# Sample attention laid out token-major on column strips, and deviations by Ln and Exp, in a hybrid encoder layer

## The chip, the cores and the metric

The kernel runs on one core of a Trainium2 chip. The metric is the device time of one launch in microseconds (us), the median of several runs. TensorE does the matrix products, VectorE, ScalarE and GpSimd the elementwise work, SyncE issues most of the transfers.

## What is computed

One layer of a hybrid encoder for 512 prompt tokens and 32 sample tokens, which share the weights. The parts that the change touches are these:

```
mod = silu(c) @ w_ada + b_ada          # c: 2 rows (prompt, sample); w_ada 1024 x 6144
a   = rmsnorm(h)*(1+sc1) + sh1 ;  a @ w_in -> retention q,k,v,gate and stick-breaking q,k,v
# stick-breaking attention, 4 heads of 128, sample: 32 queries on 1024 cached + 32 own keys
z = q.k / sqrt(128);  keep = log_sigmoid(-z), 0 where masked
A = exp(log_sigmoid(z) + sum of keep over the later keys);  out = A @ v
ret = groupnorm(retention out) * g * silu(gate)
h = h + gt1 * (concat(ret, out) @ w_out);   b = rmsnorm(h)*(1+sc2) + sh2;   then PEER(b)
```

PEER is a feed-forward part with 16384 experts and takes most of the time; the change doesn't touch it.

## The kernel before

Every engine has its own program, and semaphores order them. All activations lie feature-major (128 features on the partitions, 544 tokens along the row). A product in full precision is either fp32, which the trace shows as two instructions for each matmul, or, for the three big projections (`gemms[0]`, w_in; `gemms[1]`, w_out; `gemms[2]`, the query weights), three fp32r products of a high and a low part of weights (`whi`, `wlo`) and activations (`XH`, `XL`). GpSimd casts the high part of a weight chunk, VectorE subtracts to get the low part (`lo`). `gemm_start` works chunk 0 and 1 row block by row block, as the blocks of `XH`, `XL` become ready.

**Start.** w_ada comes in 12 groups of 512 columns. Groups 0, 2, 3 and 4 are multiplied on TensorE (`ada`, L599): 8 fp32 matmuls, whose stationary side is `siluT`, 128 rows by 2 columns, all accumulated on partitions 0 and 1. ScalarE copies the two rows (`ada_row`), and four products with `sel4` (`ada_turn`) turn them onto the partitions. Groups 1 and 5 to 11 are summed on VectorE, 16 instructions each (`ada_chunk`), and a product with ones adds the partitions (`ada_columns`). The first `gemm_start` needs the shifts and scales of groups 0 to 3, the reciprocal deviation `rs`, and the first chunk of w_in, whose load waits in the queue of SyncE for the place of group 1 (`wraw` slot 0). `ada(3)`, group 4, stands on TensorE ahead of `gemm_start`.

**Stick-breaking attention.** Prompt and sample share the engines. For a prompt head, `sb_z` makes scores, `softplus` (ScalarE: Abs, Exp, Ln) and `masked` (VectorE) make log keeps, `sb_sums` adds the suffix sums by products with a triangular matrix and with minus ones, `least` masks the diagonal, `weights` takes exponentials, `sb_out` multiplies with the values, `result` evicts. There is one tile of weights, `aw`, so `weights(h)` waits for `sb_out(h-1)`. The sample's scores lie key-major: `sample_z` makes 32 products of 32 columns, in pieces between the heads; `sample_own` the own keys. Its softplus is done once, on ScalarE ahead of `weights(3)`; then VectorE sums blocks (`rsum`), TensorE does 24 products for the suffix sums (L878 to L882), ScalarE the exponentials, and 36 products with 128 stationary columns and 32 moving ones give the output (L890). Only behind these comes `gemm_start(gemms[1])`.

**Deviations.** The group norm of retention and both RMS norms take Sqrt on ScalarE and `reciprocal` on VectorE (L1678 once for each head, L1602, L1768). The tables of ScalarE are changed from Sqrt to Ln and Exp ahead of the heads.

Of the kernel before, what the change touches and what calls it, by code (L numbers as in the profile page):

```python
# [22 lines left out]
P = 128  # L23
# [95 lines left out]
def build(nc, x_prompt, x_sample, c_prompt, c_sample, state_ret, cache_sb_k, cache_sb_v, w_ada, b_ada, norm1_g, w_in,  # L119
# [21 lines left out]
    siluT = at("siluT", o + 896, [KD, 2])  # L141
# [30 lines left out]
    sel4 = at("sel4", RT + 29184 + 640, [2])  # L172
    rows = at("rows", RT + 20480, [P])
# [6 lines left out]
    aw = at("aw", A0 + 20480, [1, 1280])  # L180
# [138 lines left out]
    s_w = [sem("s_w0"), sem("s_w1")]  # L319
    s_rowsT_ps, s_rowsT = sem("s_rowsT_ps"), sem("s_rowsT")  # L320
# [17 lines left out]
    for name, groups, reads in (("in", 7, 1), ("out", 2, 3), ("qry", 4, 1)):  # L338
# [56 lines left out]
    def _(sp):  # L395
# [22 lines left out]
        ada_load(1, 0)  # L418

        def adaw_load(g):  # L420

            if not isinstance(g, int) or g > 4:

                sp.wait_ge(*((s_ada_mm, 4) if isinstance(g, int) and g == 5 else (s_adas, 16 * (g - 4))))
            sp.dma_start(adaw[:], w_view(w_ada, g)).then_inc(s_adaw, 16)

        def gemm_loads(st, w, first_waits):

            for slot in range(2):
                sp.wait_ge(*first_waits[slot])  # L430
                sp.dma_start(wraw[:, slot], w_view(w, slot)).then_inc(s_w[slot], 16)
# [137 lines left out]
    def _(pe):  # L569
# [24 lines left out]
        def ada(n, par, w):  # L594

            if n >= 2:
                pe.wait_ge(s_adar, n - 1)
            for k in range(KD):
                last = mm(PS[0:2, 4 + par, :], siluT[:, k, :], w[:, k, :], start=(k == 0), stop=(k == KD - 1))  # L599
            last.then_inc(s_ada_mm, 1)  # L600

        def ada_turn(n, par, bank, col):

            pe.wait_ge(s_adar, n + 1)
            for x in range(4):
                last = mm(PS[:, bank, bass.ds(col + 2 * x, 2)], adar[0:2, par, x * P:(x + 1) * P], sel4[0:2, :],
                          start=True, stop=True)
# [81 lines left out]
        def gemm(st):  # L689

            def group(g, slot, first=0):
                for cc in range(first, 4):
# [4 lines left out]
                    if st is gemms[0] and cc == 1:  # L697
                        ada_columns(g + 1, slot, 7, 8 * g)
# [45 lines left out]
        ada_columns(8, 1, 7, 56)  # L744
# [69 lines left out]
        pe.wait_ge(s_gsd, NH)  # L814
# [4 lines left out]
        def sb_z(h):  # L819
            if h >= 2:  # L820
                pe.wait_ge(s_bev, h - 1)
            for kb in range(QB):
# [16 lines left out]
        def sb_out(h):  # L839
            pe.wait_ge(s_ba, 7 * (h + 1))  # L840
            for kb in range(QB):
                last = mm(zb(h, 0, kb * P, TP), svt[:, kb, h * P:(h + 1) * P],
                          aw[:, 0, pcol(kb):pcol(kb) + TP - P * kb], start=(kb == 0), stop=(kb == QB - 1))
            last.then_inc(s_bo, 1)

        def sample_z(b0):
            for b in (b0, b0 + 1):
                for h in range(NH):
                    mm(PS[:, 6 + b // 4, (b % 4) * P + h * TS:(b % 4) * P + (h + 1) * TS], kT[:, h, b * P:(b + 1) * P],
                       projT[:, SQ + h, TP:T], start=(b % 4 == 0 and h == 0), stop=(b % 4 == 3 and h == NH - 1),  # L850
                       skip_group_check=True)

        def sample_own():
            for h in range(NH):
                last = mm(PS[0:TS, 2, 256 + h * TS:256 + (h + 1) * TS], projT[:, SK + h, TP:T], projT[:, SQ + h, TP:T],
                          start=False, stop=(h == NH - 1), skip_group_check=True)
            last.then_inc(s_cz, 1)
            pe.sem_inc(gemms[1].mm, CREDIT)
# [3 lines left out]
        sample_z(0)  # L862
        sample_z(2)
        sb_sums(0)
        for h in range(NH):
            if h < 2:
                sample_z(4 + 2 * h)
            sb_out(h)
            if h < NH - 2:
                sb_z(h + 2)  # L870
            if h == NH - 2:
                sample_own()
            if h < NH - 1:
                sb_sums(h + 1)
        pe.wait_ge(s_clk, 1)
        for b in range(NPB):
            out = PS[:, 6 + b // 4, (b % 4) * P:(b % 4 + 1) * P]
            mm(out, ntri, lks[:, b, :], start=False, stop=False, skip_group_check=True)  # L878
            if b < NPB - 1:
                mm(out, negones[:], rsum[:, b, :], start=False, stop=False, skip_group_check=True)  # L880
            mm(out, negones[:], lks[:, NPB, :], start=False, stop=True, skip_group_check=True)
        mm(PS[0:TS, 2, 256:256 + P], ntri[:, 0:TS], lks[:, NPB, :], start=False, stop=True,  # L882
           skip_group_check=True).then_inc(s_cc, 1)
        pe.wait_ge(s_ca, 2)
        pe.wait_ge(s_vc, 16)
        for h in range(NH):
            hs = slice(h * P, (h + 1) * P)
            for b in range(NPB + 1):
                lhs = vraw[:, b, hs] if b < NPB else svt[:, 4, hs]
                last = mm(PS[:, 4, h * TS:(h + 1) * TS], lhs, aws[:, b, h * TS:(h + 1) * TS], start=(b == 0),  # L890
                          stop=(b == NPB))
        last.then_inc(s_co, 1)
# [178 lines left out]
    def _(act):  # L1071
# [9 lines left out]
        def squares(st, ready, b, rows=0):  # L1081
# [10 lines left out]
            act.wait_ge(st.ss, 1)  # L1092
            act_(halves(rs[:]), pair(b), ACT.Sqrt, bias=epsc[:, 0:1], scale=1.0 / D).then_inc(st.sd, 1)

        def ada_row(n, par):
# [4 lines left out]
            act_(adar[0:2, par, :], PS[0:2, 4 + par, :], ACT.Copy).then_inc(s_adar, 1)  # L1100
# [50 lines left out]
        act_(siluT[:].rearrange("p k g -> p g k"), rowsT[:, 0:16].rearrange("p (g k) -> p g k", g=2),  # L1151
# [4 lines left out]
        ada_row(2, 0)  # L1156
        for k in range(KD):
            act.wait_ge(norms[0].scaled, 2 * k + 2)
            act_(XH[:, k, :], scr1[:, k, :], ACT.Copy).then_inc(norms[0].hi, 1)
        ada_row(3, 1)  # L1160
# [28 lines left out]
        for h in range(NH):  # L1189
            act.wait_ge(s_gcen, h + 1)  # L1190
            act_(sqb[:, h, :], projT[:, h, :], ACT.Square).then_inc(s_gsq, 1)
        for h in range(NH):
            act.wait_ge(s_gv, h + 1)
            act_(halves(rsb[:, h, :]), pair(2 * h), ACT.Sqrt, bias=epsc[:, 0:1]).then_inc(s_gsd, 1)


        nc.scalar.preload_act_table_set("natural_log_exp_and_others")

        def softplus(h):
# [3 lines left out]
            if h >= 2:  # L1203
                act.wait_ge(s_bo, h - 1)
# [859 lines left out]
```

## Time and profile before

| | |
|---|---|
| median of 3 runs | 1860.61 us (1857.23 to 1862.22) |
| profiled execution | 1858.28 us, span 1856.5 us |
| instructions | 30125 |
| PE, PEld, DVE, ACT, POOL busy | 1771.3, 1697.8, 1426.0, 835.3, 564.4 us |

The span lacks 1.8 us of the execution's time, which lie around it. Times in rows are us from the start of the span. PE is TensorE's matmul side, PEld its weight loads, DVE VectorE, ACT ScalarE, POOL GpSimd, SPq the queue of SyncE.

### The profile page before, as it was taken

The numbers are of one execution on the slowest core, as the hardware profiler recorded it, in microseconds if no ns is written. First come the engines' busy times: TensorE is split into PE (matmuls) and PEld (weight loads), VectorE is DVE, ScalarE is ACT, GpSimd is POOL, SyncE is SP. The second block draws the span as 40 slices with busy tenths as digits, with TensorE's granted clock in tenths as the row PEclk, the third lists the DMA queues.
The fourth block names the chain that finished last, engine by engine and source line by source line (L and its number), as shares of the span: only waits on it lengthen the run. The fifth ranks groups of instructions, "written<-read, shape, count | busy, mean of one in ns | idle before, by whom it ended". The sixth has DMA issues, their size and how long they took to land.

```text
span 1856.5 us, 30125 instructions
## 1 busy us (share of the span) xinstructions
PE 1771.3 (95%) x11794; PEld 1697.8 (91%) x11794; DVE 1426.0 (77%) x2656; ACT 835.3 (45%) x1144; POOL 564.4 (30%) x442
## 2 busy tenths in 40 slices
PE   6999999797999999999999989998999999999998
PEld 2899986697999999999999989998899999999997
DVE  6667755435358998879878898686388988889997
ACT  2112135312125555554545545454465555555555
POOL 0111100011111524333543345434334434434320
PEclk9999999798999999999999999999999999999999
DMA  8545331032116979999999989999789999999983
GB/s 307 208 167 178 109 130 57 9 124 73 46 46 207 344 250 319 316 312 306 344 337 326 332 286 353 360 370 355 282 295 381 386 402 384 392 389 384 394 337 115
DMA packets 189217, 497.20 MB, mean 268 GB/s; under 512 B 13436, under 2 KB 76504, under 8 KB 180760
## 3 DMA queue, kind: packets, MB, share of 16 engines
q1 hardware_dynamic: 133704, 293.72, 44.4%
q0 software_dynamic: 55376, 201.61, 29.3%
q8 instruction: 91, 1.49, 0.3%
q14 instruction: 46, 0.38, 0.1%
HBM read 443.90 MB, written 51.12 MB: 267 GB/s over the span
## 4 chain that ended last, share of the span: by engine, by line
PE 82%; DVE 8%; DMA 6%; ACT 3%; issue 1%; POOL 0%; SPq 0%; DVEq 0%; ACTq 0%
PE PS L1019 24%; PE PS L574 13%; PE PS L576 12%; PE PS L575 12%; PE PS L636 5%; PE PS L970 4%; PE PS L944 3%; DMA vrw<-in_peer_v_dram 2%; DVE gat L1824 2%; DMA uraw<-in_peer_u_dram 2%; DMA gat<-in_peer_u_dram,idx 1%; PE PS L599 1%; PE PS L615 1%; PE PS L890 1%; PE PS L645 1%
## 5 line engine op out<-in xcount | busy, mean ns | idle before, releaser
L1464 POOL DMA_INDIRECT gat<-in_peer_v_dram,idx x192 | 255.1, 1329 | 368.0 <-DVE acc L1845 335.5
L1464 POOL DMA_INDIRECT gat<-in_peer_u_dram,idx x192 | 246.3, 1283 | 387.0 <-DVE a L1824 312.5
L574 PE MATMUL PS<-XH,uth 128*128 128x352 f32 x1024 | 341.6, 334 | 0.0
L1019 PE MATMUL PS<-wh,vh 128*128 128x352 f32 x1024 | 333.8, 326 | 7.6 <-DVE wl L1965 3.2
L1019 PE MATMUL PS<-wl,vh 128*128 128x352 f32 x1024 | 331.2, 323 | 0.0
L575 PE MATMUL PS<-XL,uth 128*128 128x352 f32 x1024 | 330.3, 323 | 0.0
L576 PE MATMUL PS<-XH,utl 128*128 128x352 f32 x1024 | 330.0, 322 | 0.0
L1019 PE MATMUL PS<-wh,vl 128*128 128x352 f32 x1024 | 329.6, 322 | 0.0
L1845 DVE SCALAR_TENSOR_TENSOR acc<-gat,a,acc 128x1024 f32<-128x1024 f32 x184 | 233.8, 1280 | 31.6 <-PE PS L576 27.3
L1824 DVE CUSTOM_DVE_ANT_0 gat<-gat,x 128x1024 f32<-128x1024 f32 x192 | 231.9, 1219 | 25.1 <-DMA gat<-in_peer_u_dram,idx 25.0
L574 PE MATMUL PS<-XH,whi 128*128 128x272 f32 x784 | 229.7, 293 | 10.3 <-DVE XL L1773 7.9
L576 PE MATMUL PS<-XH,wlo 128*128 128x272 f32 x784 | 228.7, 292 | 0.0
L575 PE MATMUL PS<-XL,whi 128*128 128x272 f32 x784 | 227.0, 290 | 0.0
L1329 ACT ACTIVATE vh<-vrw 128x1024 fp32r<-128x1024 f32 x128 | 135.9, 1061 | 201.0 <-PE PS L1019 182.6
L1289 ACT ACTIVATE utl<-PS 128x1024 fp32r<-128x1024 f32 x128 | 131.4, 1026 | 170.7 <-PE PS L944 170.7
L1019 PEld LDWEIGHTS PS<-wh,vh 128*128 128x128 f32 x1024 | 192.6, 188 | 11.5 <-DVE vl L1963 8.2
L1963 DVE TENSOR_TENSOR vl<-vrw,vh 128x1024 fp32r<-128x1024 f32 x128 | 156.6, 1224 | 60.0 <-ACT vh L1329 59.6
L575 PEld LDWEIGHTS PS<-XL,uth 128*128 128x128 f32 x1024 | 193.7, 189 | 5.5
L1435 POOL CAST whi<-wraw 128x1024 fp32r<-128x1024 f32 x49 | 56.0, 1145 | 469.0 <-PE PS L576 309.3
L574 PEld LDWEIGHTS PS<-XH,uth 128*128 128x128 f32 x1024 | 193.4, 189 | 5.5
L576 PEld LDWEIGHTS PS<-XH,utl 128*128 128x128 f32 x1024 | 193.2, 189 | 0.0
L1019 PEld LDWEIGHTS PS<-wl,vh 128*128 128x128 f32 x1024 | 192.7, 188 | 0.0
(294 smaller groups left out, 3182.7 us busy)
## 6 DMA issues: line engine op xcount, KB each, us to landing
uraw<-in_peer_u_dram SPq DMA_DIRECT2D x128, 512.0 KB, 5.8
vrw<-in_peer_v_dram SPq DMA_DIRECT2D x64, 1024.0 KB, 7.4
acts_dram<-gel SPq DMA_DIRECT2D x128, 176.0 KB, 6.5
gates_dram<-gst SPq DMA_DIRECT2D x22, 1024.0 KB, 10.4
al<-acts_dram SPq DMA_DIRECT2D x32, 704.0 KB, 10.4
G<-gates_dram SPq DMA_DIRECT2D x32, 704.0 KB, 9.4
adaw<-in_w_ada_dram SPq DMA_DIRECT2D x9, 2048.0 KB, 7.9
wraw<-in_w_in_dram SPq DMA_DIRECT2D x7, 2048.0 KB, 7.9
```

The source lines that it names most:

```text
L574: mm(out, ah, bh, start=start, stop=False)
L575: mm(out, ah, bl, start=False, stop=False)
L576: return mm(out, al, bh, start=False, stop=stop)
L636: last = mm(PS[:, k // 4, (k % 4) * P:(k % 4 + 1) * P], uraw[:, m % 2, k * P:(k + 1) * P], ident, start=(k % 4 == 0), stop=(k % 4 == 3), i ...
L970: last = mm(PS[:, 4 + gi % 2, x * P:(x + 1) * P], ohA[:, gi % 2, x, :], ohB[:, gi % 2, x, :], start=True, stop=True)
L1019: last = mm(PS[:, k, 0:TD], v_, w_[:, j % 2, :], start=(j == 0 and n == 0), stop=(j == NU - 1 and n == 2))
L1289: act_(utl[:, m % 2], PS[:, 0:2, :].rearrange("p b (k i) -> p (b k) i", i=P), ACT.Copy).then_inc(s_utl, 1)
L1329: act_(vh[:, j % 2], vrw[:, j // 2 % 2, j % 2, :], ACT.Copy).then_inc(s_vh, 1)
L1464: nc.gpsimd.indirect_dma_start(out=gat[:, n % NGAT, :], out_offset=None, in_=table, in_offset=bass.IndirectOffsetOnAxis(ap=idx[:, k:k + 1] ...
L1824: nc.vector.tensor_tensor_reduce(gat[:, n % NGAT, :], gat[:, n % NGAT, :], x[:], 1.0, 0.0, ALU.mult, ALU.add, a[:, k:k + 1]).then_inc(s_do ...
L1845: stt(a, row, w, old, ALU.mult, ALU.add).then_inc(s_dot, 1)
L1963: tt(vl[j % 2][:], vrw[:, j // 2 % 2, j % 2, :], f(vh[:, j % 2]), ALU.subtract).then_inc(s_vl, 1)
```

## The change

- Modulation on strips: `siluT` is 32 columns wide (30 of them zero), matmul k goes to partitions 32(k mod 4) on, and `sel4` adds the four strips when it turns. Groups 0 to 4 are all done on TensorE; group 2 has a place of its own (`adax`), loaded at the start; the 16 VectorE instructions of group 1 and its `ada_columns` are gone. Group 4's product moves behind `gemm_start`. The first w_in group is loaded in halves, ahead of it only group 3 waits in the queue. The low parts of the first two weight chunks are made before the shifts are ready.
- Sample attention: token-major, head h on partitions 32h on. The cached scores are 8 fp32 products of 512 columns, 4 heads on 4 strips. The suffix sums are one VectorE scan of 1056 columns, from the last key to the first. The weights are turned by 9 transposes; the output is 36 products on strips (32 stationary columns, 128 moving) and one transpose. All is placed between prompt heads 1 and 3.
- `aw` is two tiles; the copy `XH[0:4]` moves from ScalarE to GpSimd, ahead of the casts of w_out.
- The deviations of the group norm and of the second RMS norm become Ln and an Exp with scale -0.5; their reciprocals are gone. The first RMS norm keeps its own.

```diff
@@ start, SyncE @@
+        sp.dma_start(adax[:], w_view(w_ada, 2)).then_inc(s_adax, 16)
...
-        sp.wait_ge(s_xT, 5)
-        adaw_load(2)
         sp.wait_ge(s_ada_mm, 1)
         ada_load(3, 1)
-        sp.wait_ge(s_ada_mm, 2)
-        adaw_load(4)
-        gemm_loads(gemms[0], w_in, ((s_adas, 16), (s_ada_mm, 3)))
+        gemm_loads(gemms[0], w_in, ((s_ada_mm, 2), (s_ada_mm, 4)))
@@ start, TensorE @@
-                last = mm(PS[0:2, 4 + par, :], siluT[:, k, :], w[:, k, :], start=(k == 0), stop=(k == KD - 1))
+                q = k % 4 * 32
+                last = mm(PS[q:q + 32, 4 + par, :], siluT[:, k, :], w[:, k, :], start=(k < 4), stop=(k >= 4))
...
+        pe.wait_ge(s_w[0], 16)
+        ada(1, 1, wraw[:, 0])
+        ada_turn(0, 0, 6, 0)
         sum_once(norms[0], 1, 0)
-        pe.wait_ge(s_adaw, 16)
-        ada(1, 1, adaw)
-        ada_turn(0, 0, 6, 0)
+        pe.wait_ge(s_adax, 16)
+        ada(2, 0, adax)
+        ada_turn(1, 1, 6, 8)
         pe.wait_ge(s_w[1], 32)
-        ada(2, 0, wraw[:, 1])
-        ada_turn(1, 1, 6, 16)
-        ada_columns(1, 0, 6, 8)
-        ada_turn(2, 0, 6, 24)
-        pe.wait_ge(s_adaw, 32)
-        ada(3, 1, adaw)
+        ada(3, 1, wraw[:, 1])
+        ada_turn(2, 0, 6, 16)
+        ada_turn(3, 1, 6, 24)
         pe.wait_ge(norms[0].sd, 1)
         gemm_start(gemms[0], chunk_by_chunk(norms[0].lo, 0, lambda k: k + 1))
-        ada_turn(3, 1, 7, 0)
+        pe.wait_ge(s_adaw, 16)
+        ada(4, 0, adaw)
+        ada_turn(4, 0, 7, 0)
         gemm(gemms[0])
@@ heads, TensorE @@
-        pe.wait_ge(s_gsd, NH)
...
+        def sample_z():
+            pe.wait_ge(s_gln, NH)
...
+            for b in (1, 0):
+                if b == 0:
+                    pe.wait_ge(s_cte, 1)
+                for h in range(NH):
+                    last = mm(PS[h * TS:(h + 1) * TS, 6 + b, :], projT[:, SQ + h, TP:T],
+                              kT[:, h, b * 512:(b + 1) * 512], start=True, stop=True)
...
+                    last = mm(PS[h * TS:(h + 1) * TS, 7, 0:P], aws[:, b, h * TS:(h + 1) * TS],
+                              vraw[:, b, hs] if b < NPB else svt[:, 4, hs], start=(b == 0), stop=(b == NPB),
...
         sb_z(0)
         sb_z(1)
-        sample_z(0)
-        sample_z(2)
+        sample_z()
         sb_sums(0)
-        for h in range(NH):
...
-        pe.wait_ge(s_clk, 1)
...
+        sb_sums(1)
+        sb_out(0)
+        sb_out(1)
+        sample_turn()
+        sb_z(2)
+        sample_turn_own()
+        sb_z(3)
+        sample_out()
+        sb_sums(2)
+        pe.sem_inc(gemms[1].mm, CREDIT)
+        pe.wait_ge(s_cte, 4)
+        nc.tensor.transpose(PS[:, 6, 0:P], outs[:], ident).then_inc(s_ct, 1)
+        sb_sums(3)
+        sb_out(2)
+        sb_out(3)
@@ heads, ScalarE @@
         softplus(0)
         softplus(1)
+        softplus_sample()
         weights(0)
+        act.wait_ge(s_gln, NH)
+        act_(rsb[:], rsb[:], ACT.Exp, scale=-0.5).then_inc(s_gsd, 1)
+        weights(1)
         result(0)
+        act.wait_ge(s_cmin, 1)
+        act_(sws[:], sws[:], ACT.Exp).then_inc(s_ca, 1)
+        result(1)
+        softplus(2)
+        softplus(3)
+        weights(2)
...
@@ heads, VectorE @@
         masked(0)
+        dve.wait_ge(s_cz, 1)
+        nc.vector.tensor_copy(ownz[:], PS[:, 6, 0:TS]).then_inc(s_cte, 1)
         masked(1)
         least(0)
+        link(stt(sp8, z8, 0.0, sp8, ALU.max, ALU.add),
...
+        link(nc.vector.tensor_tensor_scan(sws[:, ::-1], ones[:, 0:1].to_broadcast([P, NS_K]), sps[:, ::-1], 0.0,
+                                          ALU.mult, ALU.add))
+        least(1)
...
+        scaled(0)
         scaled(1)
+        nc.vector.tensor_copy(aws[:, 0:NPB, :], PS[:, 6:8, :].rearrange("p b (c x) -> p (b c) x", x=P)).then_inc(s_cte, 1)
+        scaled(2)
+        nc.vector.tensor_copy(aws[0:TS, NPB, :], PS[0:TS, 6, 0:P]).then_inc(s_cte, 1)
+        scaled(3)
         masked(2)
+        dve.wait_ge(s_co, 1)
+        nc.vector.tensor_copy(outs[:], PS[:, 7, 0:P]).then_inc(s_cte, 1)
         masked(3)
         for c in range(2):
             lo(gemms[1], c, 0, c)
+        least(2)
+        least(3)
@@ second norm, ScalarE and VectorE @@
+            if st is norms[1]:
+                link(act_(halves(rs[:]), pair(b), ACT.Ln, bias=epsc[:, 0:1], scale=1.0 / D))
+                act_(rs[:], rs[:], ACT.Exp, scale=-0.5).then_inc(st.sd, 1)
+                return
...
-        link(nc.vector.reciprocal(rs[:], rs[:]))
```

## Rows read from the trace of the kernel before

**Rows 1.** The page: busy us of each engine over the span.
```profile
PE 1771.3 (95%) x11794; PEld 1697.8 (91%) x11794; DVE 1426.0 (77%) x2656; ACT 835.3 (45%) x1144; POOL 564.4 (30%) x442
```

**Rows 2.** Windows: length, busy us by engine, granted clock, DMA share, GB/s.
```profile
0.00:58.30 58.30, 43.67 (x149) 17.23 (x149) 39.40 (x59) 12.36 (x19) 4.23 (x7) 0.94 0.90 325
...
437.60:443.00 5.40, 5.38 (x24) 5.40 (x25) 5.40 (x13) 2.82 (x7) 0.00 (x0) 0.50 0.01 3
```

**Rows 3.** Chain of waits, the start: start us, us, what.
```profile
19.95 9.34 DMA adaw<-in_w_ada_dram
...
48.89 9.52 PE PS L599 x16
...
70.68 0.98 PE PS L606 x8
```

**Rows 4.** Timeline, the start: start us, us, engine, instructions.
```profile
20.85 7.03 PE L599 MATMUL PS<-wraw,siluT 128*2 128x512 f32 x16 [0.93 <-DVE hT L1583]
...
28.51 9.36 DVE L1505 SCALAR_TENSOR_TENSOR adas<-wraw,siluT,adas 128x512 f32<-128x512 f32 x14
...
41.36 5.17 DVE L1604 TENSOR_TENSOR scr<-hT,rs 128x544 f32<-128x544 f32 x8
...
50.41 1.06 POOL L1435 CAST whi<-wraw 128x1024 fp32r<-128x1024 f32 x1 [49.95 <-DMA wraw<-in_w_in_dram]
...
58.34 0.39 PE L574 MATMUL PS<-XH,whi 128*128 128x272 f32 x1
```

**Rows 5.** Transfers: of 20 to 25 us; of the tile adaw.
```profile
20.00:25.00 5.00, 4.15 (x10) 0.85 (x11) 3.49 (x6) 4.10 (x8) 0.00 (x0) 1.00 1.05 387
...
DMA to landing us min/median/max: 7.9/8.2/9.3
```

**Rows 6.** Chain of waits, the heads.
```profile
287.78 2.54 ACT rsb L1194 x4
...
292.82 1.44 ACT lk L1207 x4
...
296.88 1.70 DVE lk L1692 x4
299.55 1.91 PE PS L831 x4
...
317.22 1.71 PE PS L849 x16
318.93 2.25 PE PS L842 x8
321.85 2.42 PE PS L823 x8
...
355.30 13.33 PE PS L890 x72
```

**Rows 7.** Timeline, sample attention.
```profile
312.72 0.71 PE L831 MATMUL PS<-lk,cst 128*128 128x128 f32 x3
...
332.36 0.44 PE L855 MATMUL PS<-projT 128*32 128x32 f32 x8
...
343.11 1.22 DVE L1724 SCALAR_TENSOR_TENSOR lks<-PS,lks 128x1024 f32<-128x1024 f32 x1 [4.92 <-ACT lks L1240]
...
344.71 3.81 PE L842 MATMUL PS<-aw,svt 128*128 128x512 f32 x8 [7.39 <-ACT aw L1222]
...
368.45 0.57 PE L574 MATMUL PS<-XH,whi 128*128 128x272 f32 x1
```

**Rows 8.** Timeline, the second norm.
```profile
430.50 3.55 DVE L1768 RECIPROCAL rs<-rs 128x544 f32<-128x544 f32 x1 [0.57 <-ACT rs L1093]
...
437.62 0.57 PE L574 MATMUL PS<-XH,whi 128*128 128x272 f32 x1 [7.91 <-DVE XL L1773]
```

**Rows 9.** Groups by line: count, busy us, mean ns of one.
```profile
L599 PE MATMUL PS<-wraw,siluT 128*2 128x512 f32 x32 | 14.1, 592 | 0.9 <-DVE hT L1583 0.9
...
L878 PE MATMUL PS<-lks,cst 128*128 128x128 f32 x16 | 3.1, 275 | 0.0
```

More of the change, by code:

```diff
@@ L882, in _ @@
[L882 to L891, printed above, removed]
@@ L1156, in _ @@
         ada_row(2, 0)
+        ada_row(3, 1)
         for k in range(KD):
@@ L1233, in softplus_sample @@
+            act_(sps[:, PAST:NS_K], ownz[:], ACT.Abs).then_inc(s_ach, 1)
             chain[0] += 2
             act.wait_ge(s_ach, chain[0])
-            act_(lks[:, 0:NPB, :], lks[:, 0:NPB, :], ACT.Exp, scale=-1.0).then_inc(s_ach, 1)
-            act_(lks[0:TS, NPB, :], lks[0:TS, NPB, :], ACT.Exp, scale=-1.0).then_inc(s_ach, 1)
-            chain[0] += 2
-            act.wait_ge(s_ach, chain[0])
-            act_(lks[:, 0:NPB, :], lks[:, 0:NPB, :], ACT.Ln, bias=1.0).then_inc(s_cln, 1)
-            act_(lks[0:TS, NPB, :], lks[0:TS, NPB, :], ACT.Ln, bias=1.0).then_inc(s_cln, 1)
+            link(act_(sps[:], sps[:], ACT.Exp, scale=-1.0))
@@ L1242, in _ @@
+            act_(sps[:], sps[:], ACT.Ln, bias=1.0).then_inc(s_cln, 1)
         softplus(0)
         softplus(1)
+        softplus_sample()
         weights(0)
+        act.wait_ge(s_gln, NH)
+        act_(rsb[:], rsb[:], ACT.Exp, scale=-0.5).then_inc(s_gsd, 1)
+        weights(1)
         result(0)
-        for h in range(1, NH):
-            if h < NH - 1:
-                softplus(h + 1)
-            else:
-                softplus_sample()
-            weights(h)
-            result(h)
-            if h == 2:
-                act.wait_ge(s_gy, 4)
-                act.wait_ge(s_out, 96)
-                act_(XH[:, 0:4, :], projT[:, 0:4, :], ACT.Copy).then_inc(s_ghi, 1)
@@ L1425, in group @@
                     out = whi[:, cc % 2]
-                    if cc == 0:
+                    halved = st is gemms[0] and isinstance(g, int) and g == 0
+                    if halved and cc == 0:
+                        pool.wait_ge(s_x, 48)
+                    elif cc == (2 if halved else 0):
                         pool.wait_ge(s_w[slot], 16 * (st.before[slot] + 1) + 16 * i)
@@ L1596, in _ @@
         dve.wait_ge(s_silu, 1)
-        dve.wait_ge(s_w[0], 16)
-        for k in range(KD):
-            ada_chunk(0, 0, k, wraw[:, 0])
         dve.wait_ge(norms[0].sd, 1)
@@ L1606, in _ @@
         chain[0] += 1
+        for c in range(2):
+            lo(gemms[0], c, 0, c)
         dve.wait_ge(s_adat, 4)
@@ L1619, in _ @@
                    ALU.add).then_inc(norms[0].scaled, 1)
-            if k == 1:
-                for c in range(2):
-                    lo(gemms[0], c, 0, c)
-            if k >= 2:
-                norm1_lo(k - 2)
-        norm1_lo(KD - 2)
+            if k >= 1:
+                norm1_lo(k - 1)
         norm1_lo(KD - 1)
@@ L1708, in _ @@
+        z9 = ownz[:]
+        nc.vector.memset(aws[:, NPB, :], 0.0).then_inc(s_dch, 1)
+        chain[0] += 1
+        for h in range(NH):
+            q = slice(h * TS, (h + 1) * TS)
+            stt(ownm[q, 0, :], ntri[q, q], -1.0, ident[q, q], ALU.mult, ALU.subtract).then_inc(s_dch, 1)
+            chain[0] += 1
+        dve.wait_ge(s_dch, chain[0])
+        ts(ownm[:, 1, :], ownm[:, 0, :], -NEG, NEG, ALU.mult, ALU.add).then_inc(s_zero, 1)
         masked(0)
+        dve.wait_ge(s_cz, 1)
+        nc.vector.tensor_copy(ownz[:], PS[:, 6, 0:TS]).then_inc(s_cte, 1)
```

202 lines of the change are left out of this document (105 added, 97 removed).

## The prediction

> **What bounds the kernel now.** I read the page first: PE is busy for 1771.3 of 1856.5 us [rows 1]. So time is won only where PE waits, runs at the lower clock, or does work that is taken away. The windows then show where that is, among the stages that the diff touches. Until 58.3 us PE is busy for 43.7 us, the clock is 0.94 and the transfers take 0.90 of the time; from 437.6 to 443 us the granted clock is 0.50, the lower of its two levels, 1.2 GHz [rows 2]. The timeline adds one wait of 7.39 us in the sample's attention [rows 7]. The rest (the projections, and PEER from 520 us on) is untouched and follows on the chain, so each us won ahead of it is won at the end, and each lost is lost.
>
> The chain of waits says what sets the three places. In the start it is `ada` on PE, 7.03 us each [rows 4] and 9.52 for the last, a load between, and the turn of 0.98 us at 70.68, behind which chunk 2 of w_in begins at 71.7 [rows 3]. In the heads it goes PE, ACT, DVE, PE for each head; sample attention stands behind all, with 13.33 us of output products alone [rows 6]. `gemm_start(gemms[1])` begins at 368.45 [rows 7]. In the second norm the reciprocal takes 3.55 us on the chain [rows 8].
>
> **The price of a strip product.** This decides two of three parts, and no row shows it: before, no two neighbouring products go to different strips. An fp32 matmul of 512 columns is two instructions, 16 of them in 7.03 us, 0.44 each [rows 4]. Upper bound: the strips follow one another, 7.0 us for an `ada`, 3.5 for four score products; 36 output products of 128 columns at a quarter of the 0.88 are 7.9. Lower bound: four strips at once, 1.8 to 2.1 us for an `ada`, 1.0 for the scores; the output's 72 instructions can't go below the step of 0.055 us that eight small ones show [rows 7], so 4.0. I take the value between: the two instructions of one matmul share a strip and keep their order, so that only the second of one runs beside the first of the next; n matmuls are n+1 steps. That is 9 x 0.44 = 3.9 us for an `ada`, 5 x 0.44 = 2.2 for the scores, 37 x 0.11 = 4.0 for the output. It is a choice, nearer to the lower bound, because the operands and PSUM partitions of the strips are apart.
>
> The Trainium skill (TensorE: Matmul & The Clock Gate, Part 3) gives 2.38 times for three column strips of 512 columns and lets matmuls of different strips start within some ns. By that factor an `ada` would be an estimated 3.0 us; no run here shows it yet. The Trainium skill (TensorEngine Tiling, Key Properties) says that a change of tiling mode drains the array; that is the case against the change, and it is a rival below.
>
> **Start, with the middle price.** DVE's 16 instructions for group 1, ending at 37.87 [rows 4], go; they delayed the reciprocal. New order on PE:
> - `ada(0)` 20.85 to 24.7, `ada(1)` to 28.6 (its data is the second w_ada load, there by about 24: the last 5.4 us of the queue, below, before 29.3), turn 1.0, sum products 1.2: the sum at 30.8. Deviation on ACT 0.75, reciprocal 3.55 [rows 8], 8 scalings 5.17: DVE at 40.4 instead of 46.5 [rows 4].
> - The queue moves 387 GB/s [rows 5], 5.4 us for 2.1 MB, one after the other. `adax` lands at about 29.3, as `adaw` did [rows 3]. Group 3 is issued at 24.7, lands at 34.5; half of w_in, 2.7 us behind it, at 37.4 (before, w_in's cast began at 50.41 [rows 4]). Casts 2.1, low parts 2.5: 42.9.
> - `ada(2)` to 34.7, turn 1.0, `ada(3)` to 39.6, two turns 41.6. So DVE's low parts (42.9), not PE, release the modulation; 0.4 for shifts and scales, 2.2 to the first `XL`: `gemm_start` at 45.5 instead of 58.34 [rows 4].
> - `gemm_start` takes 12.3 us (58.34 to 70.68). But PE now idles for 3.9 us ahead of it. Where PE had idled for 7.91 us, the clock was 0.50 for the first 5.4 us [rows 2, 8], which is 2.7 us of work lost. I add 2.7 in full: 60.5.
> - `ada(4)` 3.9, copy and wait 0.7, turn 1.0: chunk 2 at 66.1 instead of 71.7. **Gain 5.6.** At the lower bound of strips the same sum gives 62.4 (gain 9.3); at the upper, 78.7 (loss 7.0: five products instead of four on PE's path).
>
> What hides here: group 5 has been loaded ahead before, and now waits for `ada(4)`. It lands 8.2 us behind its issue [rows 5], DVE sums three row blocks (3.6) and makes chunk 4's low part (1.2): 13.1 after `ada(4)`, where PE needs it at 1.7 + 12.3 (two chunks are as many products as `gemm_start`) = 14.0. Covered, by under a us; a stall of 0 to 1.5 stays in the range.
>
> **Heads and sample, with the middle price.** Until 285 us nothing changes. ACT loads Ln and Exp's table first and needs no Sqrt: four Ln at the Sqrt's price (2.54 for four, 287.78 to 290.3 [rows 6]) end at 290.3, and `sb_z(0)` waits for the second only: 289.15, 1.2 us earlier.
> - Prices: scores of a head 2.4 [rows 6]; softplus 4.0 (292.82 to 296.88); masks 2.65 (to 299.55); sums 4.5 (312.72 [rows 7] to 317.22, where L849 follows); from the last sum to `sb_out` 1.5 to 1.7 (317.22 to 318.93, with `least` and `weights`); `sb_out` 2.4; eviction to the next product 0.65 (321.2 to 321.85) [rows 6].
> - Scores 0 and 1 to 293.8. Softplus 0 to 295.7, masks to 298.4, then `ownz`. Only then the second half of the sample scores, 298.6 to 300.8: `sb_sums(0)` stands behind it, 1.2 us later than before, to 305.3. This is the one added wait; behind it on PE are both sums.
> - `sb_sums(1)` to 309.75, out 0 to 312.15, out 1 to 314.5. Before, out 1 ended at 321.2: 6.7 us won, since two weight tiles and no reciprocals of 3.55 us lie between.
> - The sample meanwhile: softplus on ACT (3.4, as the prompt's 4.0 by columns) to 304.2; DVE, behind `least(0)` (305.6), 1.2 [rows 7] and small ones to 307.2, the scan, `least(1)`, subtraction 1.5, Exp 1.1 to 314.0. Eight transposes 314.5 to 315.7. The scan has no row. Lower bound the 1.22 us of a 1024-wide instruction [rows 7]; upper bound the reciprocal's 3.55 us for 544 columns, so 6.9 for 1056. I take 1.3, the nearest kind: it ends at 308.5, before the sums of head 1 (309.75), so it is hidden; at 6.9 out 1 and all behind it is 4 us later.
> - The Trainium skill (DVE: opcode table, instruction layouts, handler registers and perf-mode slots, Feedback) says that the scan runs at half throughput; by that it would be an estimated 2.4 us, and still hidden.
> - Scores 2 to 318.0, scores 3 to 320.3; the copies of the weights on DVE (1.2, 0.25, between `scaled`) end at 318.8, hidden. Output products 320.3 to 324.3. Softplus 2 and 3 on ACT to 326.0; masks 2 to 324.6, 3 to 328.6; sums 2 324.65 to 329.15, sums 3 329.4 to 333.9, out 2 to 336.3, weights 3 to 335.4, out 3 to 338.7, eviction: `gemm_start(gemms[1])` at 339.4. DVE's two low parts of w_out (2.4) and GpSimd's copy of `XH` (2.2, 320.3 to 322.5) and its casts lie beside. ACT's rsb Exp (2.0) lies before `weights(1)`, beside `sb_out(0)`.
>
> **Gain 368.45 - 339.4 = 29.0.** What is won is the tail: 36 products of 13.33 us [rows 6], the 25 products of sums ahead of them, the 7.39 us wait of `sb_out(3)` for the sample's softplus [rows 7]. At the upper bound 344.1 (24.3); at the lower 338.3 (30.1). The other end of the clock (a stretch at 0.50 somewhere between) costs 2 to 4, and a start of the projection at full clock gives 1.4 back.
>
> **Second norm.** The reciprocal of 3.55 goes, an Exp of 0.65 comes, both ahead of all else [rows 8]: **gain 2.9.** If the Ln or Exp needed a table again, 1.3 less.
>
> **The sum.** 1858.28 - 5.6 - 29.0 - 2.9 = 1820.8. The profiled execution is 2.3 below the median of the runs shown; on that median's scale it is 1823.
>
> **The rivals.**
> - **All four strips at once.** For it: separate columns and partitions. Against: nothing here shows that two neighbouring instructions of a matmul let the next ones pass. 1858.3 - 9.3 - 30.1 - 2.9 = 1816.0, 1818 on the median's scale.
> - **Strips one after the other** (on PE the change doesn't do what it says). For it: all rows show neighbouring instructions at full steps. 1858.3 + 7.0 - 24.3 - 2.9 = 1838.1, so 1840. The start then is slower than before, the heads faster all the same.
> - **Each change of strip drains the array** (the other side). An instruction then costs its own length, not its step: 0.592 for 0.44 at 512 columns, 0.275 for 0.11 at 128 [rows 9]. Place: 80 instructions of `ada`, 16 of scores, 72 of output. Price 96 x 0.15 + 72 x 0.165 = 26.3 on top of the former: 1864.4, 1867 on the median's scale, slower by 0.3%. It decides from 0.12 us for each of the 168. Against: independent PSUM rows, and products of different banks follow at full steps today.
> - **The scan or the order of the heads stalls**: 4 us from a scan at the reciprocal's rate, 2 to 4 from a low clock: 1827 to 1831 with the middle price.
>
> **How the numbers follow.** Middle price, with or without the stall 0.40; four at once 0.29; one after the other 0.26; drain 0.03; something unseen that eats most of it 0.02. The likeliest gives 1823, its own range is 1814 to 1832. The 80% range reaches over four at once (1818, less 6 for a clock that stays up) and the serial case (1840, plus 5 for its stalls): 1812 to 1845. Within 0.3%, about what a measurement of this kernel can tell from no change, lies only the unseen case, 0.03; slower 0.03; faster 0.94.
>
> **What would show it.** A group of 16 `ada` instructions in 3.9 us (7.0: serial; 2: at once; over 9: drain). `gemm_start` of w_in near 45.5 and chunk 2 near 66; that of w_out near 339, with no wait of `sb_out` on ACT over 2 us; the scan under 2.5 us and nobody waiting for it; 5 instead of 7.9 us of idle PE in the second norm. Wrong would make it: a start past 72 us, a scan of 7 us, DVE waiting for group 5 while PE waits for chunk 4, or PE at 0.50 through the heads.

## The result, and the profile after

| | before | after |
|---|---|---|
| median | 1861.41 us (1857.23 to 1863.63, 4 runs) | 1814.26 us (1812.63 to 1817.01, 4 runs) |
| ratio, 95% interval | | 0.9749 [0.9731, 0.9767] |
| profiled execution | 1858.28, span 1856.5 | 1812.63, span 1810.8 |

The changed kernel was run again beside the last experiments, on another occasion and with its own runs of the kernel before: 1826.24 us (1824.84 to 1829.45, 5 runs) beside 1864.21, a ratio of 0.9803 [0.9783, 0.9822]. The two intervals don't meet, so by its medians the gain is known only as 38 to 47 us. The forecast (1823, 1812 to 1845) holds for both; it was made against 1860.61, so it says 0.9798.

The page after, as [rows 1]:

```profile
PE 1729.8 (96%) x11716; PEld 1670.2 (92%) x11716; DVE 1405.5 (78%) x2642; ACT 833.3 (46%) x1141; POOL 572.7 (32%) x443
```

PE is busy for 41.5 us less than in [rows 1]; its idle time (span less busy) fell only from 85.2 to 81.0.

The windows after, in the columns of [rows 2]:

```profile
0.00:28.00 28.00, 12.74 (x83) 9.01 (x84) 11.91 (x22) 7.76 (x12) 0.20 (x4) 1.00 0.88 320
28.00:36.00 8.00, 5.87 (x32) 2.13 (x34) 6.12 (x6) 1.80 (x3) 0.00 (x0) 0.75 1.06 375
36.00:46.40 10.40, 4.90 (x33) 2.31 (x25) 9.25 (x15) 1.91 (x3) 3.07 (x3) 0.66 1.07 374
46.40:52.20 5.80, 5.80 (x26) 5.80 (x27) 5.80 (x15) 2.72 (x5) 0.00 (x0) 0.50 1.07 414
...
395.50:400.00 4.50, 4.50 (x20) 4.50 (x21) 4.50 (x11) 2.37 (x5) 0.00 (x0) 0.50 0.00 0
```

From 28 to 46.4 us PE is busy for only 10.8 of 18.4 us, the granted clock falls to 0.75 and 0.66 on average, and the first 5.8 us of `gemm_start` run at 0.50. At the second norm the clock is 0.50 too, as in [rows 2].

The chain of waits after, the start (as [rows 3]):

```profile
5.21 18.13 DMA wraw<-in_w_ada_dram
23.38 1.97 PE PS L611 x16
25.36 13.04 DMA wraw<-in_w_in_dram
38.55 1.05 POOL whi L1463
39.62 4.04 DVE wlo L1528 x2
...
46.37 0.57 PE PS L585
...
61.39 1.90 PE PS L611 x16
63.31 0.61 ACT adar L1133
63.96 1.05 PE PS L618 x8
```

Two loads, a cast and the low parts now carry the start; of PE's products only 1.97 us are on the chain ahead of `gemm_start`, where [rows 3] has 9.52 for the last `ada` alone. The turn of group 4 (`ada_turn`) ends, and chunk 2 begins, at 65.02.

The timeline after, heads and second norm (as [rows 4, 7, 8]):

```profile
20.90 1.92 PE L611 MATMUL PS<-wraw,siluT 128*32 128x512 f32 x16 [0.79 <-DVE hT L1619]
...
291.79 1.93 PE L873 MATMUL PS<-kT,projT 128*32 128x512 f32 x8 [3.65 <-DVE ownz L1749]
293.65 1.67 PE L846 MATMUL PS<-lk,cst 128*128 128x128 f32 x4
...
300.60 2.36 DVE L1758 TENSOR_TENSOR_SCAN sws<-ones,sps 128x1056 f32<-128x1056 f32 x1
...
312.75 1.96 PE L897 MATMUL PS<-vraw,aws 128*32 128x128 f32 x64
...
317.32 1.14 PE L846 MATMUL PS<-lk,cst 128*128 128x128 f32 x4 [2.40 <-DVE lk L1726]
...
333.10 0.36 PE L585 MATMUL PS<-XH,whi 128*128 128x272 f32 x1 [0.73 <-ACT projT L1256]
...
391.26 0.66 ACT L1124 ACTIVATE rs<-rs 128x544 f32<-128x544 f32 x1
...
395.49 0.56 PE L585 MATMUL PS<-XH,whi 128*128 128x272 f32 x1 [5.01 <-DVE XL L1815]
```

An `ada` takes 1.92 us where [rows 4] has 7.03; two of the five, under the fallen clock, take 3.40 and 3.56. The scan takes 2.36 and ends before head 1's sums do: ScalarE waits 1.58 us for the masks behind it, PE for nothing. `gemm_start` of w_out begins at 333.10 instead of 368.45, that of the queries at 395.49 instead of 437.62.

### The profile page after: what moved, and what is told of

Its sections match the earlier page's. It is cut to its first block, busy times and chain, and to the rows that moved or that the text cites. A ratio compares the mean times of both kernels' runs of the same rounds, so it can differ in the third digit from the quotient of the medians.

```text
span 1810.8 us, 29957 instructions
## 1 busy us (share of the span) xinstructions
PE 1729.8 (96%) x11716; PEld 1670.2 (92%) x11716; DVE 1405.5 (78%) x2642; ACT 833.3 (46%) x1141; POOL 572.7 (32%) x443
## 3 DMA queue, kind: packets, MB, share of 16 engines
q0 software_dynamic: 55376, 201.61, 30.1%
## 4 chain that ended last, share of the span: by engine, by line
PE 80%; DVE 8%; DMA 7%; ACT 3%; issue 1%; POOL 0%; SPq 0%; DVEq 0%; ACTq 0%; POOLq 0%
PE PS L1048 23%; PE PS L585 13%; PE PS L587 13%; PE PS L586 13%; PE PS L648 5%; PE PS L999 4%; PE PS L973 3%; DMA vrw<-in_peer_v_dram 2%; DVE gat L1866 2%; DMA uraw<-in_peer_u_dram 2%; DMA gat<-in_peer_u_dram,idx 1%; DMA wraw<-in_w_ada_dram 1%; DVE vl L2005 1%; PE PS L657 1%; DMA wraw<-in_w_in_dram 1%
## 5 line engine op out<-in xcount | busy, mean ns | idle before, releaser
L1497 POOL DMA_INDIRECT gat<-in_peer_v_dram,idx x192 | 262.5, 1367 | 359.7 <-DVE acc L1887 323.4
L1048 PEld LDWEIGHTS PS<-wh,vl 128*128 128x128 f32 x1024 | 192.8, 188 | 0.0
## 6 DMA issues: line engine op xcount, KB each, us to landing
al<-acts_dram SPq DMA_DIRECT2D x32, 704.0 KB, 10.6
```

The lines of the kernel that those rows point to most:

```text
L1048: last = mm(PS[:, k, 0:TD], v_, w_[:, j % 2, :], start=(j == 0 and n == 0), stop=(j == NU - 1 and n == 2))
L1497: nc.gpsimd.indirect_dma_start(out=gat[:, n % NGAT, :], out_offset=None, in_=table, in_offset=bass.IndirectOffsetOnAxis(ap=idx[:, k:k + 1] ...
```

## The experiments

Eleven new kernels, and the changed one once more. Three have a single part of the change, eight are the changed kernel with a few lines edited. Their whole times scatter, so each is read first by stages of its trace: `rsb` is the start of the group norm's Sqrt or Ln on ACT, "out" `gemm_start` of w_out, "last" the start of VectorE's last group of evictions of w_out (three instructions), "query" `gemm_start` of the query weights. Ratios are to the kernel before, run beside. The last kernel, with products added to price strips, ran once (1865.41 us) and is read by its trace alone.

| kernel | median, ratio to before | rsb | rsb to out | out to last | last to query | query to end |
|---|---|---|---|---|---|---|
| before | | 287.78 | 80.67 | 55.82 | 13.35 | 1418.9 |
| after | 0.9749 | 281.06 | 52.04 | 52.93 | 9.46 | 1415.3 |
| start alone | 1852.72, 0.9954 | 280.52 | 80.70 | 56.03 | 13.35 | 1421.5 |
| heads alone | 1829.72, 0.9823 | 285.96 | 50.60 | 54.45 | 12.69 | 1424.2 |
| norm 2 alone | 1857.43, 0.9982 | 285.89 | 81.76 | 56.18 | 10.46 | 1422.1 |
| `ada` on one strip | 1834.72, 0.9842 | 296.64 | 50.64 | 54.46 | 10.45 | 1423.7 |
| output by heads | 1820.54, 0.9782 | 280.46 | 53.64 | 52.95 | 9.46 | 1419.3 |
| own scores first | 1818.46, 0.9766 | 280.56 | 49.45 | 54.42 | 9.45 | 1418.2 |
| added products | 1812.66, 0.9742 | 278.91 | 50.58 | 54.46 | 9.47 | 1417.8 |
| cast held back | 1818.39, 0.9765 | 279.59 | 51.52 | 54.46 | 10.45 | 1421.1 |
| after, again | 1826.24, 0.9803 | 280.21 | 50.64 | 52.94 | 9.46 | 1429.8 |
| three edits | 1816.50, 0.9744 | 278.00 | 49.51 | 54.44 | 9.47 | 1422.1 |
| one weight tile | 1829.36, 0.9815 | 280.12 | 57.23 | 52.92 | 9.46 | 1426.1 |

**The parts alone (three kernels).** Each is the kernel before with the hunks of one part of the diff.

> The kernel before with the start part alone (strips in the modulation, its loads, the early low parts); heads and deviations as before. Theory (the gains of the parts are separate and add up): chunk 2 of w_in begins at 65.0 us instead of 71.7, and the end moves by the same 6.6 us, 1854.8 us, with nothing more in PEER. Rival (part of the 3.4 us that PEER gave in the whole change comes from how the start shifts everything behind it): the end moves by 8 to 10 us, 1852, with the excess between 1064 and 1339 us of the trace.

> The kernel before with the heads part alone (sample attention on strips, the scan, two weight tiles, the order, the group norm's deviation by exponentials, the copy on GpSimd). Theory: gemm_start of w_out comes 28.6 us earlier, at 339.8 us, and the projection behind it begins at full clock and gives 2.9 more by its end; together 31.5 us, 1829.9 us. Rival (the clock in the projection came from the start, not from the heads): 28.6 us, 1832.8. Second rival (PEER's 3.4 us belong to the heads): 34.9 us, 1826.5.

> The kernel before with the second RMS norm's deviation by Ln and Exp alone. Theory: an Exp of 0.66 us for a reciprocal of 3.55 us on the chain, 2.9 us, 1858.5 us. Rival (the shorter wait keeps TensorE at the higher clock for longer): 3.9 us, 1857.5. Rival (the table has to be loaded between Ln and Exp): 1.6 us, 1859.8.

Start 0.9954 [0.9937, 0.9970], heads 0.9823 [0.9794, 0.9852], norm 0.9982 [0.9966, 0.9999]. Their product is 0.9760, between the two ratios of the whole: the parts add up as far as this can tell. By medians they give 7.7, 30.7 and 3.0 us, where 6.6, 31.5 and 2.9 were expected; the interval of the third alone is 3 us to either side. In the stages the start is 5.4 us ahead of the two other kernels that lack it; the heads alone reach "out" in 50.6 us instead of 80.7 to 81.8, and the norm alone "query" in 10.46 instead of 13.35. None of the three explains PEER: "query to end" is 1421.5 to 1424.2 in them, and in the unchanged kernel after it is 1415.3 once and 1429.8 once.

**The changed kernel again.**

> The changed kernel once more, unchanged, as the measure of what two executions of the same kernel differ by. The profiled execution of the first was 1812.6 us and its stretch behind the start of the query projection 1415.3 us, where seven other kernels that don't differ there took 1417.8 to 1424.2. Theory (the 3.4 us that PEER seemed to give were chance): this stretch takes 1417 to 1424 us here. Rival (they came from the change): 1414 to 1416.

1429.8 us for the stretch behind "query": outside what either theory expected. Its size differs by 14 us between two traces of one program, so the 3.4 us that the first pair of traces showed there can't be put down to the change, and most of what lies between 0.9749 and 0.9803 lies in this stretch as well. But it isn't plain scatter from one execution to the next: the four runs of the first occasion lie within 4.4 us, the five of the second within 4.6, and the two groups 7.8 us apart, while the kernel before moved by only 2.8. The experiments were run on three chips, and for the first result none is on record; whether the chip makes the difference is not shown. In the trace, PE's waits for the transfer `uraw` in PEER are 10.0 us in the first and 12.9 in the second, those of L1008 for VectorE's queue 2.5 and 6.8.

**Strips off in the modulation.**

```diff
-                q = k % 4 * 32
-                last = mm(PS[q:q + 32, 4 + par, :], ..., start=(k < 4), stop=(k >= 4))
+                last = mm(PS[0:32, 4 + par, :], ..., start=(k == 0), stop=(k == KD - 1))
```

> The changed kernel with all eight matmuls of each modulation product on one strip (partitions 0 to 31), all else kept. Theory (four strips at once carry the start): 7.0 us for a product instead of 1.9; the sum of squares comes at 37.0 instead of 27, group 3's product ends at 51, gemm_start of w_in begins at 56 instead of 46.4, and chunk 2 at 77 instead of 65.0, less up to 2.7 us because TensorE stays busy ahead of gemm_start and may keep its clock: 9 to 12 us slower, 1823.5 to 1826.5 us. Rival (loads and low parts set the start, so strips hardly matter): gemm_start moves by under 3 us, 1815 to 1818.

Timeline of this kernel:

```profile
37.11 7.05 PE L610 MATMUL PS<-adax,siluT 128*32 128x512 f32 x16
...
56.83 0.57 PE L585 MATMUL PS<-XH,whi 128*128 128x272 f32 x1 [2.83 <-DVE XL L1647]
...
79.46 1.05 PE L617 MATMUL PS<-sel,adar 32*128 32x2 f32 x8 [0.68 <-ACT adar L1132]
```

`gemm_start` is 10.5 us later, the turn of group 4 15.5 (63.96 after), `rsb` 15.6; the ratio 0.9842 is 17 us above 0.9749, but only 7 above 0.9803, so the stages are the better witness. The rival that loads alone set the start falls. The expectation, 9 to 12, was short by 3.5 at its upper end. `gemm_start` here ran at 0.50 as well, in spite of 2.83 us of waiting only:

```profile
36.00:44.00 8.00, 8.00 (x21) 2.35 (x20) 5.93 (x5) 1.18 (x2) 0.00 (x0) 1.00 1.00 333
44.00:56.80 12.80, 10.00 (x41) 4.50 (x41) 10.21 (x15) 2.49 (x4) 4.37 (x3) 0.97 0.59 215
56.80:62.60 5.80, 5.78 (x25) 5.80 (x26) 5.80 (x15) 2.65 (x5) 0.00 (x0) 0.50 1.05 425
```

**Strips off in the output, by order alone.**

```diff
-            for b in range(NPB + 1):
-                for h in range(NH):
+            for h in range(NH):
+                for b in range(NPB + 1):
```

> The changed kernel with the output products of the sample's attention in another order: nine of a head one after the other on its strip, then the next head, where neighbours were on four strips. Same instructions. Theory (strips run at once only where neighbours are on different ones): the 72 instructions take 7.9 us instead of 2.2, and the first 2.4 us of the 5.7 more are hidden, since TensorE waited that long for VectorE's masks behind them; gemm_start of w_out comes 3.3 us later, 1817.5 us. Rival (a small product's time is its own overhead, strips don't matter): 2.2 us, 1814.3.

The 72 instructions take 6.8 us instead of 2.2, and 7.9 were expected; so neighbours on other strips are what makes them fast. But the sums of head 2 begin only 6.76 us behind the first of them, against 4.57 after: 2.2 later instead of the 3.3 expected, for 2.4 of the 4.6 were hidden. And from there to "out" it is 14.09 us (320.01 to 334.10) against 15.78 (317.32 to 333.10) in both traces of the changed kernel. The reason stands in the windows; after:

```profile
318.00:320.00 2.00, 2.00 (x8) 1.65 (x7) 1.44 (x4) 0.53 (x1) 2.00 (x3) 0.67 1.05 410
320.00:322.00 2.00, 2.00 (x5) 1.10 (x4) 1.97 (x7) 0.00 (x0) 0.89 (x1) 0.50 1.03 384
```

and with the order by heads:

```profile
316.00:320.00 4.00, 4.00 (x45) 3.81 (x43) 1.74 (x7) 2.97 (x4) 0.00 (x0) 1.00 0.00 0
320.00:324.00 4.00, 4.00 (x18) 2.87 (x18) 3.85 (x9) 0.00 (x0) 3.07 (x3) 1.00 0.66 227
```

Fast products leave a wait of 2.40 us, behind which the clock here falls to 0.50; with slow ones it stayed. But the fall doesn't always follow. Ten traces have this wait, and in six of them the clock stays at 1.00 behind it, as with `ada` on one strip:

```profile
333.18 1.14 PE L845 MATMUL PS<-lk,cst 128*128 128x128 f32 x4 [2.40 <-DVE lk L1725]
```

There it is 14.10 us to "out" (347.28). So four strips in the output are worth 2.2 us where the clock stays (six traces) and 0.5 where it falls. (The stage of 53.64 in the table has another stretch at 0.50 in it, from 290 to 296 us.)

**A strip by itself.** Groups of this kind, one line each:

```diff
+            for k in range(8):
+                mm(PS[k // 2 * 32:k // 2 * 32 + 32, 6, :], s32, wide, start=True, stop=True)  # pairs
```

> The changed kernel with groups of fp32 products that nobody reads ahead of the second norm's sum, behind busy TensorE, to price strips by themselves: 8 matmuls of 512 columns (16 instructions) on one strip, alternating on two, in pairs (0,0,1,1,..), on four; 9 on three; 8 of full width; 4 full ones alternating with 4 on strips; 36 of 128 columns on one strip and on four. Theory (a strip is a queue of its own; only neighbours on the same strip follow each other): 7.0, 3.5, 5.7, 1.75 us; three 2.6; full 7.0; alternating with full 7.0; 36 small ones 7.9 on one and 2.0 on four. Rival (each change of the width of the product drains the array): the alternating group takes 16 x 0.59 = 9.5 us.

Timeline; L605 one strip, L607 two, L609 pairs, L611 three, L613 four, L615 full, L617 and L618 full and strip in turn, L620 and L622 small ones on one and on four:

```profile
389.07 6.63 PE L605 MATMUL PS<-cst 128*32 128x512 f32 x15
...
395.56 4.00 PE L607 MATMUL PS<-cst 128*32 128x512 f32 x15
399.40 1.94 PE L609 MATMUL PS<-cst 128*32 128x512 f32 x16
401.11 2.35 PE L611 MATMUL PS<-cst 128*32 128x512 f32 x15
...
403.33 2.28 PE L613 MATMUL PS<-cst 128*32 128x512 f32 x15
405.54 7.13 PE L615 MATMUL PS<-cst 128*128 128x512 f32 x16
412.51 1.02 PE L617 MATMUL PS<-cst 128*128 128x512 f32 x2
413.46 1.04 PE L618 MATMUL PS<-cst 128*32 128x512 f32 x2
414.44 1.12 PE L617 MATMUL PS<-cst 128*128 128x512 f32 x2
415.50 1.04 PE L618 MATMUL PS<-cst 128*32 128x512 f32 x2
...
427.37 2.21 PE L622 MATMUL PS<-cst 128*32 128x128 f32 x69
```

A row's length contains the 0.6 us of its last instruction, and the rows overlap, so groups are priced from start to start. On one strip instructions follow at a step of 0.43 (6.63 less 0.6, over 14), as at full width. One strip and two together take 10.33 us (389.07 to 399.40): 6.9 for 16 instructions on one, so 3.4 on two. Pairs take 1.71 (399.40 to 401.11). Three and four together take 4.43 (401.11 to 405.54), where a step of 0.43 for each three and each four instructions makes 2.6 + 1.7; the change to full width behind them adds 0.1. The 72 small ones take 7.8 us on one strip and 2.0 on four. So n strips are n times as fast, up to four. The Trainium skill (TensorE: Matmul & The Clock Gate, Part 3) gives three strips 2.38 times; here it is 3 times by the steps.

Two things came out unlike expected. Pairs (0, 0, 1, 1, ...) take as long as four strips in turn and not 5.7 us: with four instructions a strip, those of the next strips don't wait for them. With 18 a strip, in the experiment before, most did. And where full and 32-column products alternate, a change costs: the starts of the groups of two are 0.95 to 1.06 us apart, on average 1.01, where two steps are 0.86. That is 0.15 a change, as much as lies between an instruction's length and its step [rows 9]; the 16 instructions take 8.1 us, between the 7.0 of the theory and the 9.5 of the rival, which counted a drain for each instruction. The Trainium skill (TensorEngine Tiling, Key Properties) says that a change of tiling mode drains the array; by that the measured 0.15 would be such a drain, and changes from strip to strip, which keep the mode, cost none, as here.

**The added wait.** VectorE's copy `ownz` goes ahead of `masked(0)`.

> The changed kernel with VectorE's copy of the sample's own scores ahead of the masks of head 0 instead of behind them. In the trace TensorE waited 3.65 us for this copy, and the second half of the scores and the sums of head 0 stood behind it, so the sums began 1.9 us after the masks were done. Theory (this wait lies on the path through the heads): gemm_start of w_out 1.9 us earlier, 1812.4 us. Rival (ScalarE or VectorE would be waited for instead, 2 us later): no change, 1814.3.

The wait of 3.65 us is gone; the sums of head 0 begin at 291.18, 10.6 us after `rsb`, against 12.6 after and 11.7 in the second run of it. "rsb to out" is 49.45 against 52.04 and 50.64. So the wait cost 1.2 us, where 1.9 were expected, and a further 1.4 in the first run, where the clock behind it was 0.50 for a stretch; behind the same wait of 3.66 us the second run had 1.00. Of the nine traces with this wait it is the only one without the fall.

**One tile of weights again.** `weights` and `least` wait for `s_bo >= h`, all heads use one tile.

> The changed kernel with one tile of weights for all four heads, so that the masks and exponentials of a head wait for the output of the one before, as in the kernel before. Theory (the second tile shortens both pairs of heads): the least, weights and output of heads 1 and 3 stand 1.8 us later each, gemm_start of w_out 3.6 us later. Rival (other work fills it, the scan in the first pair above all): under 1 us later.

From `sb_out` 0 to the transposes behind `sb_out` 1 it takes 6.84 us instead of 4.40, from `sb_out` 2 to "out" 7.68 instead of 5.22 (second run of after): 4.9 us together, more than the 3.6 expected: PE idles 2.25 and 2.19 us ahead of the second `sb_out` of each pair, where masks and exponentials begin only behind the first. The remaining 1.7 of the table's 6.6 come from a stretch at 0.50, between 292 and 296 us, that the second run of after lacks.

**Filling the waits.** 3 and 6 matmuls of 512 columns in the start, 3 and 5 around the second norm's sum, as `mm(PS[:, bank, :], ident, cst[:, 0:512], ...)`; then the held-back cast; then both with `ownz` first.

> The changed kernel with products added that nobody reads, in TensorE's waits only: 3 and 6 fp32 matmuls of 512 columns around the modulation's last product ahead of gemm_start of w_in, 3 and 5 around the sum of squares of the second norm. Theory (the granted clock of 0.50 at the head of both projections follows from the waits ahead of them): both projections begin at 1.00, 2.7 us won at each, 1809 us; if the clock of the start stays at 0.50 in spite of them, the added products at 0.85 us an instruction overrun and gemm_start of w_in comes up to 6 us later, 1817. Rival (the clock at these places has another cause): granted clock 0.50 as before, no gain at either, 1814 or more.

> The changed kernel with GpSimd's cast of weight chunk 2 of w_in held back until all low parts of the activations are made. In the trace VectorE's two low parts of chunks 0 and 1 took 4.04 us beside GpSimd's casts, where two took 2.36 without, and they released the shifts. Theory (casts beside them slow VectorE down, and this lies on the path of the start): 3.0 us for the two, gemm_start of w_in 1.0 us earlier, 1813.3 us. Rival (the transfers, which share of time was 1.06 there, slow it): 4.0 us and 1814.3.

> The changed kernel with the three edits together: own scores copied first, added products in TensorE's waits, cast of chunk 2 held back. By the traces of each alone 2.6 us in the heads, 2.1 in the start and 2.7 at the second norm from the added products, and 0.6 from the cast: 8.0 us less than the changed kernel run beside it, ratio to it 0.9956. Rival (what is won in the start is taken back, since loads set it): 5 us, 0.9972.

Windows with the added products, at both heads of projections:

```profile
46.90:52.00 5.10, 5.06 (x40) 5.09 (x41) 5.10 (x13) 2.59 (x4) 0.00 (x0) 1.00 1.06 404
393.40:400.00 6.60, 6.58 (x49) 6.25 (x49) 6.60 (x17) 3.74 (x9) 0.00 (x0) 1.00 0.00 0
```

The clock is 1.00 at both, here and in the kernel with all three edits, where every other trace of this start has a stretch at 0.50 at the head of `gemm_start`; so its fall did follow from PE's waits. What it gives is less than 2.7 each: in the start the turn of group 4 at 61.81 instead of 63.96 and 63.11 (1.3 to 2.2), in the norm 12.24 us from "query" to the first eviction instead of 13.89 (1.65), because VectorE makes one of the eight `XL` blocks each 1.65 us and PE now goes at that pace.

With the cast held back the two low parts take 3.17 us instead of 4.04, and `gemm_start` is at 45.79, 0.6 to 0.8 earlier. But the 3.17 alone prove nothing: four traces without this edit have it too, and there the cast takes 2.13 us instead of 1.05, and the shifts behind it come 0.6 later. So cast and subtraction get in each other's way, and sometimes the one is stretched, sometimes the other. From the first low part to `gemm_start` it is 6.47 to 6.75 us in eight traces without the edit and 5.86 in the two with it. The rival, transfers, falls: in "own scores first" the second low part takes 1.21 us at a transfer share of 1.05.

All three together ran beside the second run of after: 1816.50 to 1826.24, ratios 0.9744 [0.9719, 0.9768] to 0.9803 [0.9783, 0.9822]. That is 0.9940 (+-0.003, from the two half-widths), against the 0.9956 expected. Yet the stages don't bear the expected 8.0 us out: `rsb` is 2.2 us earlier, "rsb to out" 1.1 shorter, "out to last" 1.5 longer, 1.8 in all at "query", and 1.65 are won behind it. That is 3.5 us; the other 6 lie in the last stretch, which no edit touches behind that point. So it was faster than the changed kernel beside it, by 3.5 us that the trace accounts for.

## Why the prediction held, step by step

- **The price of a strip product** is the step that failed, though the total held. The middle price (3.9, 2.2 and 4.0 us) was wrong: four strips run at once, 1.92 us for an `ada` ([rows 4] for before), 1.04 for four score products at full clock, 2.2 for the output. The output's lower bound was wrong too: 72 instructions went under the step of 0.055 us that was taken for a floor, with 0.03 on average. So the case held likeliest (0.40) had the wrong mechanism and its rival (0.29) the right one; their totals, 1823 and 1818, lie too close for the measured 1814 and 1826 to tell them apart. The traces do.
- **The start** gave 6.0 us: `rsb` at 280.5 (mean of six traces whose start is that of the change) against 286.5 (three without). Predicted were 5.6, and 9.3 for four strips at once, which supposed that PE would be on the path. The sequence was right: low parts, not PE, release the shifts. `gemm_start` came at 46.37 against 45.5, chunk 2 at 65.02 against 66.1, since `ada(4)` took 1.9 and not 3.9. But the agreement is partly luck. DVE's two low parts took 4.04 us beside the casts and not 2.5, while the prediction's own sum had a slip that made up for 0.9 of it: 37.4 + 2.1 + 2.5 is 42.0, not 42.9. The 9.52 us of the last `ada` before, from which it counts, are PE at work with the clock at 0.51 from 47.1 to 54.1 us; the two other traces of that start have 8.7 and 8.5, and their turn of group 4 ends at 69.8 and not 71.7. And the 0.50 at the head of `gemm_start`, priced at 2.7 us, held for 5.8 us and more in the first trace only; in the seven others of this start the first 5.8 us have a mean of 0.57 to 0.72. The stall for group 5 didn't come: PE's longest wait from 65 to 280 us is 0.4 us.
- **Heads:** "rsb to out" fell from 81.0 (three traces) to 51.0 (four: after twice, heads alone, one strip in `ada`), 30.1 against the 29.0 of the middle and 30.1 of the four-at-once price. That equality is partly luck: each of these traces has one or two stretches at 0.50 in it, which the sum lacks, and the scan took 2.36, not 1.3. The scan stayed hidden, as said. The Trainium skill (DVE: opcode table, instruction layouts, handler registers and perf-mode slots, Feedback) gives half throughput, an estimated 2.4 us; the trace agrees. The one added wait was priced at 1.2 and measured at 1.2. Of the mechanisms named for the gain, two were measured by themselves: the second tile 4.9, the output's strips 0.5 to 2.2. That the wait of 7.39 us for the softplus is gone is seen in the trace; its share wasn't measured.
- **The projection of w_out** gave 2.3 us that the sum lacks: "out to last" 56.0 before, 52.9 or 54.4 after. Before, the clock is 0.51 for its first 3.1 us and again from 385.0 to 388.6; now PE is busy ahead of it and it begins at 1.00. The prediction mentioned 1.4 for this in a clause and left it out of the sum. The second stretch, 1.5 us, stands behind a wait of 2.34 us and comes and goes: all three traces with the old heads and seven of eleven with the new ones have it (54.4), four don't (52.9).
- **Second norm:** 2.9 predicted. It gave 2.9 alone, and 3.9 in the two traces of after, where the sum product ahead of it had the full clock (1.18 us where it was 2.18). No table was loaded between Ln and Exp.
- **The sum:** 6.0 + 30.1 + 2.3 + 3.3 ("last to query", 13.1 in three traces without the change to the norm, 9.8 in after twice and the one-strip kernel) = 41.7 us, against 37.5 predicted and 38.0 and 47.2 measured by medians. The rest lies behind "query", where the kernels are the same.
- The **drain** rival doesn't hold: changes of strip cost nothing that shows. A cost of 0.15 us exists, but between widths, of which this change has few. The sentence of the Trainium skill on a change of tiling mode, which the prediction put beside this rival, excepts a change of the tile alone, and so never spoke for it.

## What to carry to other kernels

Spread small-output fp32 products over column strips wherever they lie side by side, also when it takes zero padding; the gain is 3.7 times on the product, but what it is worth is set by the next thing on the path, and by TensorE's clock, which may fall in the wait that the faster product leaves. Price a change by stage spans of several traces, not by one whole time: here a stretch that no edit touches moved by 14 us between two traces of one program. A second tile between two engines that hand a buffer back and forth was worth more (4.9 us) than the faster output products behind it (0.5 to 2.2 us).

## What the runs showed of the hardware

- fp32 products on four column strips run at once: 16 instructions of 512 columns in 1.92 us instead of 7.03. From start to start, one, two, three and four strips take 6.9, 3.4, 2.3 and 1.7 us for 16 (that of three from 2.6 for 18). The order may be in pairs (1.71 us), but not in 18s (6.8 us for what takes 2.2).
- 128-column products on four strips start 0.03 us apart on average, on one strip 0.11.
- A change between full-width and 32-column products costs 0.15 us; between strips, nothing that shows.
- The same wait is not always followed by the same clock. Behind the one of 3.65 us a granted clock of 0.50 came in eight of nine traces, behind one of 2.40 us in four of ten, behind one of 2.34 us in ten of fourteen. So losses of 1.4 to 1.7 us come and go.
- A cast on GpSimd beside a subtraction on VectorE (both 128x1024) stretches one of the two: the subtraction from 1.21 to 2.02 us and more, or the cast from 1.05 to 2.13.
